# Decoder step with a routed expert layer: routing groups of 4, 3 and 2 tiles, and token rows weighted by POOL and ACT

## What is computed

```python
x = x + cross_attn(rmsnorm(x, g_x), mem_k, mem_v, w_xq, w_xo)
n = rmsnorm(x, g_ffn)
g_idx  = argmax(n @ w_rg + b_rg)                    # 1 of 4 groups
e_sel  = (n @ w_re + b_re)[g_idx]                   # 8 experts of that group
top_v, top_i = top_k(e_sel, 2)
gates  = softmax(top_v) * softmax(group logits)[g_idx]
for each expert e:                                  # 32 of them
    y += (silu(n @ w_e1[e]) * (n @ w_e3[e]) * gates[:, e]) @ w_e2[e]
x = x + y; output = rmsnorm(x, g_final)
```

## Time and profile before

| | us |
|---|---|
| median of 3 runs | 1067.43 (1067.07 to 1067.89) |
| the profiled execution | 1065.81 |
| its span, first to last instruction | 1064.0 |
| PE busy, share of the span | 999.0, 94% |
| DVE busy | 638.3, 60% |
| ACT busy | 541.6, 51% |
| POOL busy | 197.6, 19% |

### The profile page before, as it was taken

One profiled execution on the slowest core, in us unless ns is written; L12 is line 12 of the kernel. 1 busy time (PEld: TensorE's weight loads), 2 busy tenths in 40 slices (PEclk: granted clock), 3 DMA queues, 4 the chain that ended last, 5 costly groups with the idle time before them and its releaser, 6 DMA issues. The chain is left out here.

```text
span 1064.0 us, 14237 instructions
## 1 busy us (share of the span) xinstructions
PE 999.0 (94%) x5327; PEld 848.1 (80%) x5327; DVE 638.3 (60%) x1175; ACT 541.6 (51%) x918; POOL 197.6 (19%) x136
## 2 busy tenths in 40 slices
PE   8999999999999999999999999948999999999970
PEld 6998999798887689999655878847888888888850
DVE  4526756345654650002664125677999999999935
ACT  6644333305221532213545012255999999999944
POOL 0003211100000021200000300011333375642220
PEclk9999999999999999999999999967999999999995
DMA  9701111244000653103563005487999999999738
GB/s 314 217 1 59 57 42 40 99 139 173 1 1 0 225 177 113 40 20 127 232 256 139 1 37 201 159 310 300 396 392 391 384 364 390 382 387 393 284 55 335
DMA packets 55211, 203.06 MB, mean 191 GB/s; under 512 B 10710, under 2 KB 19423, under 8 KB 41575
## 3 DMA queue, kind: packets, MB, share of 16 engines
q1 hardware_dynamic: 44327, 181.61, 44.9%
q0 software_dynamic: 10816, 20.54, 7.6%
HBM read 185.06 MB, written 32.83 MB: 205 GB/s over the span
## 5 line engine op out<-in xcount | busy, mean ns | idle before, releaser
L527 PE MATMUL bank<-regA_r,regW_r 128*128 128x352 f32 (+1 forms) x456 | 148.8, 326 | 0.0
L526 PE MATMUL bank<-regA_r,regW_r 128*128 128x352 f32 (+1 forms) x456 | 148.7, 326 | 0.0
L359 POOL TENSOR_TENSOR regW_r<-regW,regW_r 128x1024 fp32r<-128x1024 f32 x19 | 47.1, 2477 | 348.7 <-ACT regW_r L346 348.6
L1525 ACT ACTIVATE regY_r<-expert_w 128x1024 fp32r<-128x1024 f32 x105 | 108.9, 1062 | 1.0 <-PE bank L527 0.9
L525 PE MATMUL bank<-expert_w_r,regS_r 128*128 128x512 f32 x256 | 103.4, 404 | 0.0
L1525 ACT ACTIVATE regW_r<-expert_w 128x1024 fp32r<-128x1024 f32 x87 | 90.2, 1061 | 6.7 <-PE bank L527 6.7
L2292 DVE TENSOR_TENSOR expert_w_r<-expert_w,regY_r 128x1024 fp32r<-128x1024 f32 x74 | 89.0, 1218 | 0.0
L525 PE MATMUL bank<-regY_r,regW_r 128*128 128x352 f32 (+1 forms) x264 | 87.3, 331 | 0.5 <-ACT regB L1206 0.5
L526 PEld LDWEIGHTS bank<-regA_r,regW_r 128*128 128x128 f32 x456 | 85.9, 188 | 0.4
L527 PEld LDWEIGHTS bank<-regA_r,regW_r 128*128 128x128 f32 x456 | 85.6, 188 | 0.0
L2466 POOL DMA_INDIRECT regW<-normed_tokens,idx x32 | 44.0, 1374 | 200.0 <-DVE idx L2201 119.6
(11 more groups left out here) (363 smaller groups left out, 2408.1 us busy)
## 6 DMA issues: line engine op xcount, KB each, us to landing
expert_w<-in_we SPq DMA_DIRECT2D x96, 1024.0 KB, 13.3
regY<-in_cache_mem_v SPq DMA_DIRECT2D x6, 1024.0 KB, 7.2
regW<-in_wbc SPq DMA_DIRECT2D x11, 512.0 KB, 3.6
regS<-in_x_prompt SPq DMA_DIRECT2D x8, 512.0 KB, 6.5
regX<-in_x_prompt SPq DMA_DIRECT2D x8, 512.0 KB, 6.6
regW<-in_wq SPq DMA_DIRECT2D x8, 512.0 KB, 3.6
regA<-in_kct SPq DMA_DIRECT2D x4, 1024.0 KB, 7.9
token_sums<-regX SPq DMA_DIRECT2D x8, 512.0 KB, 2.9
```

Of the source, the lines that this page charges most:

```text
L359: eng.tensor_tensor(lo, raw, hi.bitcast(F32), ALU.subtract).then_inc(w_lo[name], 1)
L526: nc.tensor.matmul(out, stays[1], moves[0], start=False, stop=False)
L527: ins = nc.tensor.matmul(out, stays[0], moves[0], start=False, stop=last)
L1525: nc.scalar.activation(part_hi[u % HI], part_raw[n % RAW], ACT.Copy).then_inc(m_wh, 1)
```

## The change

- Routing groups become tiles 0 to 3, 4 to 6, and 7 to 8 (`ROUTED`). `route(0)` follows the copy of tile 4, `route(1)` that of tile 7, `place(0)` that of tile 6. `place(1)` stands behind the residual, copy and `rstd` of tile 8. On PE `ranks(0)` moves to round 6, `slots(0)` to round 8, and `ranks(1)` behind `tx_sum(8)`.
- `normed_rows` and `weighted_rows` leave DVE. POOL multiplies each row by the gain into `xn2` once the sum of squares is out (two operations of 512 columns, signal `s_weighted`). ACT scales it by the row's factor (`scaled_rows(t - 1)`, behind ACT's copy of tile t), and the store waits for that. For tile 8 ACT takes the square root behind `scaled_rows(7)`.
- POOL's load of `oix` now comes behind its nine multiplications.
- Parts 7 and 8 wait for the landing of the first gather (`m_g[0]`).
- Some scratch areas move; `listed_gates` now lies where tile 8's row is stored from, so `gates` waits for that store to land.

```diff
-GT = 3
+ROUTED = [(0, 4), (4, 7), (7, NT)]
+GT = 4
@@ PE
-                if t in (5, 8):
-                    ranks((t - 5) // 3)
-                if t == 7:
+                if t == 6:
+                    ranks(0)
+                if t == 8:
                     slots(0)
...
             tx_sum(NT - 1)
+            ranks(1)
             router(NT - 1)
@@ SP
             part_load(4)
+            sp.wait_ge(m_g[0], 16)
             for p in range(7, 9):
                 part_load(p)
@@ ACT
+            def scaled_rows(t):
+                r = rows_of(t)
+                act.wait_ge(s_weighted, t + 1)
+                act.wait_ge(s_rooted, t + 1)
+                nc.scalar.activation(xn2[0:r, t % 2], xn2[0:r, t % 2], ACT.Copy,
+                                     scale=stat[0:r, 140 + t:141 + t]).then_inc(s_xn[3], 1)
...
+                if t < NT - 1:
+                    root_3(t)
                 if t >= 3:
                     filled(act, ("R", t - 3))
                 ps, sg = filled(act, ("T", 3, t, 1))
                 copy(YT3[t % 3][:, 4:8, 0:r], ...)
+                if t > 0:
+                    scaled_rows(t - 1)
+            root_3(NT - 1)
+            scaled_rows(NT - 1)
@@ DVE
                 if t < NT - 1:
                     rstd(3, t)
+                    nc.vector.sem_inc(s_rooted, 1)
                     if t > 0:
                         add_bias(t - 1)
-                    normed_rows(t)
-                else:
-                    weighted_rows(t)
...
-                if t in (3, 6):
-                    route(t // GT - 1)
                 if t in (4, 7):
-                    place(t // GT - 1)
+                    route((t - 4) // 3)
+                if t == 6:
+                    place(0)
+            rstd(3, NT - 1)
+            nc.vector.sem_inc(s_rooted, 1)
             add_bias(NT - 2)
-            rstd(3, NT - 1)
-            nc.vector.sem_inc(s_last, 1)
+            place(1)
             add_bias(NT - 1)
             route(2)
             place(2)
...
                 link(tt(w2, w1, dif, ALU.mult))
+                dve.wait_ge(s_xnd[0], 16 * 5)
@@ POOL
+            for t in range(NT):
+                r = rows_of(t)
+                if t >= 2:
+                    g.wait_ge(s_xnd[t % 2], 16 * (t // 2))
+                for h in range(2):
+                    emptied(g, ("O2", t, h))
+                if t < NT - 1:
+                    g.wait_ge(s_sq[3], t + 1)
+                for q in range(2):
+                    ins = g.tensor_tensor(xn2[0:r, t % 2, 512 * q:512 * q + 512], X[0:r, t, 512 * q:512 * q + 512],
+                                          grow[q][0:r, :], ALU.mult)
+                ins.then_inc(s_weighted, 1)
```

More of the change, by code:

```diff
@@ L237, in trunk_step @@
         rank_of = v3(regS, 1216, 2 * GT, NE)
[L238 to L243, removed]
+        ranks_of = [small[:, 24 + 2 * t0:24 + 2 * t1] for t0, t1 in ROUTED]
+        table_tmp = [lgm[:, 2 * GT * k:2 * GT * (k + 1)] for k in range(5)]
+        gix = regS[:, 1472:1472 + GT]
+        gone = v3(regS, 1476, GT, NG)
+        own = v3(regS, 1492, GT, NE)
+        esel = v3(regS, 1620, GT, EPG)
         re_ = v3(wpool, 0, 8, NE)
@@ L844, in slots @@
                     take(("PL",), 2)
-                for j in range(2 * GT):
+                t0, t1 = ROUTED[b_]
+                for j in range(2 * (t1 - t0)):
                     ins = nc.tensor.matmul(bank[2][:, 0:2 * NE].rearrange("p (c e) -> p c e", c=2),
                                            at_slots[b_][:, j, :], listed[:, j],
-                                           start=(b_ == 0 and j == 0), stop=(b_ == NT // GT - 1 and j == 2 * GT - 1))
-                if b_ < NT // GT - 1:
+                                           start=(t0 + j == 0), stop=(2 * t0 + j == 2 * NT - 1))
+                if t1 < NT:
                     ins.then_inc(s_slotd, 1)
@@ L1495, in _, with root_3 @@
                 hi_of(act, ("XB", k))
+            def root_3(t):
+                r, c = rows_of(t), 120 + t
+                act.wait_ge(s_sq[3], t + 1)
+                nc.scalar.activation(stat[0:r, c + 10:c + 11], stat[0:r, c:c + 1], ACT.Sqrt,
+                                     scale=1.0 / D, bias=small[0:r, 0:1]).then_inc(s_rt[3], 1)
+            def scaled_rows(t):
[4 more added lines that the diff above has]
+                                     scale=stat[0:r, 140 + t:141 + t]).then_inc(s_xn[3], 1)
             for t in range(NT):
@@ L2063, in route @@
             def route(b_):
-                tiles = range(GT * b_, GT * b_ + GT)
-                lg = lgm[:, LG * GT * b_:LG * GT * (b_ + 1)].rearrange("p (t c) -> p t c", t=GT)
-                u = ui[:, :].rearrange("p (t c) -> p t c", t=GT)
+                t0, t1 = ROUTED[b_]
+                n, tiles = t1 - t0, range(t0, t1)
+                lg = lgm[:, LG * t0:LG * t1].rearrange("p (t c) -> p t c", c=LG)
+                u = ui[:, 0:16 * n].rearrange("p (t c) -> p t c", t=n)
+                group, chosen, mine, best = gix[:, 0:n], gone[:, 0:n], own[:, 0:n], esel[:, 0:n]
                 for j, t in enumerate(tiles):
```

129 lines of the change are left out of this document (58 added, 71 removed).

## The result

| | before, same chip | changed |
|---|---|---|
| median of 6 runs, us | 1067.57 (1065.69 to 1070.19) | 1076.32 (1073.19 to 1077.72) |
| ratio, 95% interval | | 1.0067 [1.0055, 1.0078] |
| profiled execution | 1065.81 | 1076.83 |
| its span | 1064.0 | 1075.0 |

The change makes the kernel slower, by 7.2 us if the ratio is put on 1067.6. On the 1067.43 us of the prediction that is 1074.6; forecast were 1072.3, between 1064.8 and 1075.5. The ratio is the one on record with its interval, and not the quotient of the two medians, which is 1.0082: the medians lie 8.75 us apart, and 1076.32 itself is above the forecast's range. The direction and the mechanism came out, the size was too small.

A forecast was written before the change was run, and what follows sets the result against it. The landing of the first gather, which starts `ab(0)` on PE, was taken to bound the kernel. Rows 5.0 us later, less 0.1 for `slot_gates`, made 1067.43 + 4.9 = 1072.3 us; range 1064.8 to 1075.5.

The forecast's parts named there:

- DVE held by POOL: In each tile's `rstd`, DVE operations on SBUF tensors stand still beside POOL's multiplications: `rstd` ends 1.9 us later per tile.
- The stalls: PE waits 1.8 us for the residual of tile 5 and 2.2 us for the copy ahead of its router.
- T(7): Start of the transposes of tile 7 on PE: 2.7 us later than 692.90, near 695.6.
- From that landing to the rows at PE: Tile 8's store lands at 720.6, gather issues to about 722.0, part 4 is ahead until 723.5, rows land at 724.6.
- (a): Parts 7 and 8 no longer ahead of the first gather: it lands at 716.8 rather than 719.6, 2.8 us.
- (b): DVE loses two operations of 0.75 us a tile, 1.4 us with overlap; PE waits for it only at tile 8.
- (c): `place(1)`, 2.1 us, no longer stands ahead of the residual of tile 8, for which PE was 0.8 us late.
- (d): `route(2)` on DVE has two tiles, not three: 3.9 us instead of 5.0.
- (1): DVE hardly held: tile 8's store lands at 714.6, rows at 718.8, -0.8 us, total 1066.6; chance 0.23.
- (2): DVE not held and the DMAs land tile 8's store before 712.7: gather gains 2.4 us, total 1065.0; chance 0.20.
- (3): All five operations of `rstd`, and those of `route`, held beside POOL: 1.4 us more, total 1073.7; chance 0.12.
- Its own marks: Signs: three `rstd` operations at 1 us or more, two PE stalls, T(7) near 695.6, loads near 707, gather released by store.

The follow-up runs named there:

- POOL short: The changed kernel with POOL multiplying only the first 32 of each 512 columns, waits and order kept: 1070.47 us, 1.0031.
- POOL later: The changed kernel with POOL's multiplications of a tile waiting until DVE has finished that tile's root (`s_rooted`): 1068.99 us, 1.0011.
- the kernel with rows on DVE with and without its stall filled: The changed kernel with row weighting given back to DVE: 1068.4 us, 1.0008; with five unread products in PE's wait before tile 5's router: 1065.93 us, 0.9978.
- the changed kernel with its stall filled: The changed kernel with eight unread products on PE in the wait ahead of the router of tile 5: 1073.49 us, 1.0045.
- loads ahead of it: The changed kernel with weight parts 5 and 6 issued ahead of tile 7's row store: 1074.13 us in 4 runs, 1.0062.
- loads alone: The kernel before, with only parts 7 and 8 made to wait for the first gather: 1065.22 us, 0.9979.
- both repairs: The changed kernel with POOL waiting for DVE's root and parts 5 and 6 issued ahead of tile 7's row store: 1068.15 us, 0.9997.

## Why the prediction was right, and where its sizes failed

- **What bounds it**: right. The end moves with the first gathered rows (the table above).
- **DVE held by POOL**: right in kind and nearly in size. Predicted +1.9 us for `rstd`, measured +1.6: L1661 and L1649, with one input, passed, L1650 took what was left of POOL's first operation, L1651 all of the second. The prediction set a rule of the Trainium skill beside this ("SBUF — State Buffer", section "SBUF: two separate sides": a lock against operations with two SBUF inputs or in a 2-port mode). The trace agrees for these four: 0.15 and 0.17 us for the single-input ones against 0.73 and 1.20. POOL short gives back 0.0036 of the ratio and POOL later 0.0056: the hold, with the stalls and the clock behind it, is half of the loss or more.
- **The stalls**: at the places named. Ahead of tile 5 0.98 us, not 1.8; ahead of its router 2.01, against 2.2.
- **T(7)**: predicted 695.6, measured 697.51. Tile 4 was 0.66 us late in this execution, the round of tile 4 was 0.5 shorter, and from tile 5 to tile 6 it took 12.3 us instead of 10.5. **This is the step that failed: the walk left PE at full clock behind a stall.** From 684 to 687.5 us products took 0.63 us instead of 0.39, and the granted clock was half. With the same wait ahead of the router or the products that fill it, and the clock at 1.00, the round took 10.7 us, so the fall cost 1.6; the kernel with rows on DVE with and without its stall filled, and the changed kernel with its stall filled, show what the fall costs.
- **From T(7) to the residual of tile 8**: 8.6 us, predicted 8.7. The three loads left 3.15 us behind that, predicted 2.7, and from them to the landing of tile 8's store it took 14.0, predicted 13.6. That the store and not `idx` sets the gather came true in the changed kernel; loads ahead of it changed the releaser.
- **From that landing to the rows at PE**: predicted 4.0, measured 5.8. The second term mis-sized. I read only the first of the gather's two issues; with nothing ahead the two and the landing take 4.25 us from POOL's start (loads alone), and with part 4, sent at 722.51, ahead of them 5.5.
- **Sum at the rows**: 724.6 predicted, 729.00 measured. The 4.4 us are 1.9 (T(7)), -0.1, 0.45, 0.4 and 1.8 in the order above. That the forecast is only 2.3 us short by the ratio is in part luck: by the rows it is 4.4 short, and by the medians 4.0.
- **(a) the later loads**: 2.2 us instead of 2.8, probably since the gather's second issue shortens what could be won; no run separates that. But in the changed kernel this gain is hidden: part 4 is still ahead of the gather, late with everything else.
- **(b), (c), (d)**: what DVE was spared bought nothing. With rows on DVE, the groups and the order, (c) and (d), gave 1.0008, and 0.9978 when the stall of their longer `route(0)` was filled, no better than the loads alone. (b) is not in those two kernels; with both repairs all three are there, at 0.9997, no better either.
- **Rivals**: (1) DVE hardly held, 1066.6: what this would have looked like is POOL short, at 1.0031 or 1070.7 in those units, so its price was 4 us too low, for the same two reasons at the gather (landing at 716.4, not 714.6, and 5.9 us from there to PE). (2) is excluded: the store landed at 723.2 here and at 716.4 without the hold, not by 712.7. (3), all five operations of `rstd` held, is refuted by the rows; its 1073.7 lies nearer to the measured time by luck, since its extra 1.4 us stand in for the clock and the gather's second issue, which neither sum had.
- **Its own marks**: of the three operations named, L1651 reached 1 us, L1650 (0.73) and L1652 (0.16) did not; the rest of the list came true except T(7)'s number and the time of the loads (709.2, not 707).

## What to carry to other kernels

Work moved to an idle POOL is not free when PE waits for a chain of small DVE operations on SBUF tensors: beside two multiplications of 1.3 us, a chain of five operations of 0.16 us each took 1.6 us longer. Put POOL's part where DVE reads PSUM; moving it by one semaphore gave back 0.6% here. Price a new PE stall at its length and, as a risk, a clock at half speed behind it, 1.6 us here; and when a queue's item is delayed, look at what big transfers are delayed with it and land in front of the next urgent one.

## What the runs showed that I had not expected

- A PE stall of 1.3 to 2.0 us in an otherwise dense stretch was followed by a stretch at 1.2 GHz, though PE was busy again. In the changed kernel it began near 684.1, PE having resumed at 682.47, and ended at 687.5 (granted clock 0.50, product 0.63 us instead of 0.39):

```profile
686.00:687.00 1.00, 1.00 (x4) 0.81 (x3) 0.97 (x2) 0.00 (x0) 0.88 (x1) 0.50 0.00 0
...
680.00:690.00 10.00, 7.99 (x39) 6.50 (x39) 5.25 (x11) 1.46 (x4) 3.40 (x3) 0.83 0.27 107
```

  With a stall of 2.04 us at the same place the clock stayed at full speed in the profile of the kernel with the loads ahead. Five products of no use in a stall of 1.32 us were worth 0.3% of the kernel.
- DVE gets in between two POOL operations that are ready back to back, for one operation: L1650 finished at the border, L1651 was held for all of the second (1.20 us of 1.28).
- An operation with one input was held too: L2093, a cast of three elements, 0.67 us beside POOL instead of 0.17, while L1661 and L1649 passed. Why these differ isn't settled by any run here.
- The landing of one 256 KB store behind the same three loads of 1 MB took from 9.5 to 11.7 us in five kernels, with 287 to 336 GB/s on the mean from the loads to that landing; I had taken one number for it.
- Starting the experts 2.4 us earlier left 0.5 us at their end in one profile.
